# Low weight parts of the late units on VectorE instead of GpSimd

## The chip, the cores and the metric

The kernel runs on one core of a Trainium2 chip. The metric is the device time of one execution in microseconds. A core has TensorE (PE in the profile), VectorE (DVE), ScalarE (ACT), GpSimd (POOL) and SyncE (SP), which here only issues DMA transfers. Each engine works through its own instructions in order and waits on semaphores.

## What is computed

One inference step of a hybrid convolutional decoder layer for 1024 prompt tokens, 16 meta tokens and 8 sample tokens, all in fp32 with a width of 1024:

```
proj = rmsnorm(h) @ w_in                 # 1024 -> 9 * 1024 columns
u_a  = a_val * sigmoid(a_glu);  c_a = layernorm(causal_conv31(u_a) + bias)
y_a  = silu(c_a) * silu(a_gate)
u_b  = b_c * b_h;               y_b = b_b * causal_conv3(u_b) * silu(b_gate)
merged = sigmoid(m_a) * (y_a @ w_pa) + sigmoid(m_b) * (y_b @ w_pb)
h = h + merged @ w_out;         y = rmsnorm(h)
```

## The kernel before

**Units.** The projections are cut into 44 units of 256 output columns: unit 0, then eight rounds of "glu", "short" and "gate" (units 1 to 24), the late units 25 to 35 (gates whose results go to DRAM), "pb" units 36 to 39 (y_b @ w_pb) and "pa" units 40 to 43 (y_a @ w_pa). After them comes the output projection (L2173).

**Seven products.** A unit's 2 x 2 block product over halves of rows, columns and the sum is done as a Strassen-Winograd form with seven products instead of eight, called slots 0 to 6. Each product has 24 matmuls, since each fp32 operand is split into a high part (rounded to fp32r) and a low part (what the rounding left), and high x high, high x low and low x high are summed. The results are evacuated and combined by ScalarE (L1103, L1133, L1148) and VectorE: `c11` (L1664), `c22` (L1670), `c12` (L1675) and `after_c21`.

**Weights.** Six steps n = 0 to 5 prepare the weights of a unit v during unit v - 1: step n makes the high part on ScalarE (`w_hi`, L980, once the slot's product of the unit before is done) and the low part on GpSimd (`w_lo`, L913: raw minus high, 128x512, and 128x1024 for n = 3, which fills slots 3 and 4). The raw blocks lie in `ring`: rb11, rb21, rb22 are loaded (L448, L456, L473), and u1 to u4 are sums. Up to unit 26 the sums are made by accumulating DMAs that GpSimd issues; from unit VSUM = 27 on VectorE makes them in `weight_sum` (L1657). Each low part counts up the semaphore `wlo`, on which TensorE waits before a slot, and SyncE before it loads a ring buffer again.

**Order on SyncE.** All loads and spills stand in one hand-written queue. In a pb unit u (m = u - 36) its order is: u13 of unit u + 2 (L438), spills of the last unit (L620, L624; the latter waits for `after_c21` of that unit), `load_sgb(m, 0)` (L603), rb11 (L448, waits for `wlo` of step 0 of unit u + 1), `load_sg2` (L608), rb21 (L456, waits for step 1), `load_sgb(m, 1)` (L603), a spill, `load_sgb(m, 2)` (L603, waits until the buffer was read), rb22 (L473, waits for step 4), a spill (L616).

**Sigmoids of pb units.** ScalarE copies each sgb load into PSUM (`stage_sigmoids`, L1170) and stands in order between its other work: stage (m, 0) before the third product's evacuation (L1133), stage (m, 1) before the fourth's (L1148). VectorE multiplies with them in `after_c11` (L1682), `after_c22` (L1696) and `after_c12` (L1720). TensorE's slot 4 waits for L1133, slot 5 for L1148, slot 6 for `c22`.

**Phase changes.** Around units 35/36 and 39/40 the moving operand changes as well: ScalarE makes high parts (L996), and VectorE sums (`x_sum`, L1499) and low parts (`x_low`, L1462).

Of the kernel before, what the change touches and what calls it, by code (L numbers as in the profile page):

```python
# [34 lines left out]
def decoder_step(nc, x_prompt, x_sample, state_conv_a, state_conv_b, meta_tokens, norm_g, w_in, conv_a_w,  # L35
# [37 lines left out]
    NZ, NPB, NU = 36, 40, 44  # L73
# [29 lines left out]
    def w_at(v, n):  # L103
        return n + 1 if v == 0 else 6 * v - 2 + n + 1
# [8 lines left out]
    VSUM = LATE0 + 2  # L113
# [4 lines left out]
    def ring_at(v):  # L118

        return v // 2 + v % 2  # L120
# [52 lines left out]
    with ExitStack() as ctx:  # L173
# [6 lines left out]
        def sem(name):  # L180
            return ctx.enter_context(nc.semaphore(name))
# [65 lines left out]
        def f(ap):  # L247
            return ap.bitcast(F32)
# [39 lines left out]
        whi, wlo, prod, snap, ev = sem("whi"), sem("wlo"), sem("prod"), sem("snap"), sem("ev")  # L288
# [66 lines left out]
        def w_step(v, n):  # L355

            if v == 0:
                s = (0, 1, 3, 5)[n]
                return (rb11, rb21, u13[0][:, 0, :], rb22)[n].unsqueeze(1), s, s + 1
            if n == 3:  # L360
                return u13[v % 2], 3, 5
            s = (0, 1, 2, None, 5, 6)[n]
            return (rb11, rb21, u2, None, rb22, u4)[n].unsqueeze(1), s, s + 1
# [513 lines left out]
        @block.gpsimd  # L877
        def _(pool):
            G = nc.gpsimd
            G.memset(eps[:, 0:1], RMS_EPS)  # L880
            G.memset(eps[:, 1:2], LN_EPS).then_inc(pool_const, 1)
            G.memset(ident[:, :], 0.0).then_inc(pool_const, 1)
            G.memset(ones[:, :], 1.0 / D).then_inc(pool_const, 1)
            pool.wait_ge(pool_const, 3)
            G.affine_select(out=ident[:, :], in_=ident[:, :], compare_op=ALU.not_equal, fill=1.0, base=0,
                            pattern=[[-1, P]], channel_multiplier=1).then_inc(pool_const, 1)


            def u1_sum(v):
                pool.wait_ge(rb11_in, 16 * (v + 1))  # L890
                pool.wait_ge(u13_in[v % 2], u13_at(v))
                G.dma_start(u13[v % 2][:, 0, :], rb11, accum_op=ALU.add).then_inc(a1[v % 2], 16)  # L892

            def u2_sum(v):
                pool.wait_ge(u2_in, 16 * v)
                pool.wait_ge(a1[v % 2], 16 * ring_at(v))
                G.dma_start(u2, u13[v % 2][:, 0, :], accum_op=ALU.add).then_inc(a2, 16)  # L897

            def u3_sum(v):
                pool.wait_ge(rb22_in, 16 * (v + 1))  # L900
                pool.wait_ge(u13_in[v % 2], u13_at(v))
                G.dma_start(u13[v % 2][:, 1, :], rb22, accum_op=ALU.add).then_inc(a3[v % 2], 16)

            def u4_sum(v):
                pool.wait_ge(u4_in, 16 * v)
                pool.wait_ge(a2, 16 * v)
                G.dma_start(u4, u2, accum_op=ALU.add).then_inc(a4, 16)

            def w_lo(v, n):

                pool.wait_ge(whi, w_at(v, n))
                raw, s0, s1 = w_step(v, n)
                G.tensor_tensor(wop[:, s0:s1, 1, :], raw, f(wop[:, s0:s1, 0, :]), ALU.subtract).then_inc(wlo, 1)  # L913

            for n in range(4):
                w_lo(0, n)

            u1_sum(1)
            u3_sum(1)
            u2_sum(1)  # L920
            u4_sum(1)
            u1_sum(2)
            u2_sum(2)
            pool.wait_ge(wlo, w_at(1, 5))

            for u in range(1, NU):
                v = u + 1
                if u > 1:
                    w_lo(u, 5)
                if v < NU:  # L930
                    w_lo(v, 0)
                if v < VSUM:
                    u3_sum(v)
                if v < NU:
                    w_lo(v, 1)
                if v < VSUM:
                    u4_sum(v)
                if v < NU:
                    w_lo(v, 2)
                if v + 1 < VSUM:  # L940
                    u1_sum(v + 1)
                if v < NU:
                    w_lo(v, 3)
                if v + 1 < VSUM:
                    u2_sum(v + 1)
                if v < NU:
                    w_lo(v, 4)


# [491 lines left out]
        def _(dve):  # L1441
# [56 lines left out]
                                     (q[0], q[3], q[0], ALU.subtract), (q[1], q[0], q[1], ALU.add))[n]  # L1498
                V.tensor_tensor(out, x, y, op).then_inc(xsum, 1)  # L1499

            def w_low(n):

                dve.wait_ge(whi, w_at(1, n))
                raw, s0, s1 = w_step(1, n)
                V.tensor_tensor(wop[:, s0:s1, 1, :], raw, f(wop[:, s0:s1, 0, :]), ALU.subtract).then_inc(wlo, 1)

            normalize(0)
# [129 lines left out]
            def weight_sum(v, n):  # L1637

                u1, u3 = u13[v % 2][:, 0, :], u13[v % 2][:, 1, :]
                if n == 0:  # L1640
                    dve.wait_ge(rb11_in, 16 * (v + 1))
                    dve.wait_ge(u13_in[v % 2], u13_at(v))
                    dve.wait_ge(wlo, w_at(v - 2, 3))
                    if v - 2 < VSUM:
                        dve.wait_ge(a2, 16 * (v - 2))
                else:
                    dve.wait_ge(usum, usum_at(v, (0, 0, 0, 1)[n]))
                if n == 1:
                    dve.wait_ge(rb22_in, 16 * (v + 1))
                    dve.wait_ge(wlo, w_at(v - 1, 2))  # L1650
                    if v - 1 < VSUM:
                        dve.wait_ge(a4, 16 * (v - 1))
                if n == 3:
                    dve.wait_ge(rb21_in, 16 * (v + 1))
                    dve.wait_ge(wlo, w_at(v - 1, 5))
                out, x, y = ((u1, rb11, u3), (u2, u1, rb22), (u3, u3, rb22), (u4, u2, rb21))[n]
                V.tensor_tensor(out, x, y, ALU.add).then_inc(usum, 1)  # L1657
# [69 lines left out]
            def after_c21(u):  # L1727
                kind, i = UNITS[u]
                if kind in ("short", "pb", "pa"):
                    dve.wait_ge(prod, prod_at(u, 6))  # L1730
                b = psum_half(u, 6)
                if kind == "glu":
                    dve.wait_ge(glu_ready, 2 * i + 2)
                    dve.wait_ge(ev, snap_at(u, 2))
                    if i == 0:
                        dve.wait_ge(xlo, 12)
                        V.memset(ua[:, 0:LEAD], 0.0).then_inc(lead_zero, 1)
                        dve.wait_ge(lead_zero, 1)
                    else:
                        dve.wait_ge(conv_step, CONV_OPS * i)  # L1740
                        dve.wait_ge(conv_act, 3 * i)
                        dve.wait_ge(tail_ready, 2 * i)
                        dve.wait_ge(sa_in, 2 * i)
                    V.tensor_tensor(ua[:, LEAD:LEAD + ALL], g0, g1, ALU.mult).then_inc(ua_ready, 1)
                elif kind == "short":
                    dst = half(g3, u, 1)
                    V.tensor_tensor(dst, b, dst, ALU.mult).then_inc(ub_ready, 1)
                elif kind == "gate":
                    dve.wait_ge(bswish_ready, 2 * i + 2)
                    dve.wait_ge(yb_step, 2 * i + 1)  # L1750
                    V.tensor_tensor(g2[:, META:ALL], g2[:, META:ALL], g0[:, META:ALL], ALU.mult).then_inc(yb_step, 1)
                elif kind == "pb":
                    dst = g3[:, HY:TOK].rearrange("p (c w) -> p c w", w=CY)
                    dve.wait_ge(sg2_in, 16 * i + 16)
                    V.tensor_tensor(dst, b, dst, ALU.mult).then_inc(pb_step, 1)
                elif kind == "pa":
                    halves = [t[:, HY:TOK].rearrange("p (c w) -> p c w", w=CY) for t in (merged_pair(i), old_pair(i))]
                    merge(u, 3, halves[0], b, halves[1])
# [54 lines left out]
            for u in range(1, NU):  # L1813
                kind, i = UNITS[u]
                n = late(u)
# [8 lines left out]
                    w_low(5)  # L1824
                if u > 1:
                    after_c21(u - 1)
                if VSUM <= u + 1 < NU:
                    weight_sum(u + 1, 0)
                if kind == "gate":
# [26 lines left out]
                if VSUM <= u + 1 < NU:  # L1856
                    for step in (1, 2, 3):
                        weight_sum(u + 1, step)
                if kind == "gate":
                    sample_b(i)  # L1860
                if spread:
# [43 lines left out]
                if u == LAST:  # L1905
                    wo_low(3)
                after_c22(u)
                if kind == "short":
                    sample_a(i)
                if spread:  # L1910
# [12 lines left out]

                c12(u)
                after_c12(u)
                if spread:
                    conv_a(cb, steps[2], steps[3])
                    if steps[3] == CONV_OPS:
                        c_sum(cb)
# [287 lines left out]
```

## Time and profile before

| | |
|---|---|
| median of 3 runs | 1082.22 us (1081.83 to 1085.32) |
| the profiled execution | 1079.23 us |
| its span, first to last instruction | 1077.4 us |
| TensorE busy | 1027.6 us, 95% of the span |
| VectorE busy | 838.0 us, 78% |
| GpSimd busy | 521.6 us, 48% |
| ScalarE busy | 469.3 us, 44% |

A row of a timeline gives the start, the time taken, engine, line, operation, output and input, and in brackets how long the engine stood idle before it and what ended that. SPq is SyncE's queue. "x24" is the number of instructions that a row merges; one product has 24 matmuls. An idle time "<-issue" is one whose releaser the profile doesn't name.

### The profile page before, as it was taken

Reading aid. Unit: us, or ns where it says so; the run is one execution under the profiler, and the core shown is the slowest. Engines: PE = TensorE matmul, PEld = TensorE weight load, DVE = VectorE, ACT = ScalarE, POOL = GpSimd, SP = SyncE. Lnnn points to the kernel's source line nnn. Section 1 sums busy time; section 2 is a strip of 40 time slices with the busy share of each in tenths; the row PEclk is TensorE's granted clock in tenths of the full one; section 3 lists DMA queues with packets and bytes.
Section 4 is the critical chain, followed back from the end, with each engine's and each line's share of the span. In section 5 each row is a group of like instructions: output and inputs, shape, how many; then the busy total and the mean of one; then the engine's idle time right before and its main releaser. Section 6 shows DMA issues by size and latency. Waiting matters only on the chain.

```text
span 1077.4 us, 19843 instructions
## 1 busy us (share of the span) xinstructions
PE 1027.6 (95%) x7948; PEld 998.9 (93%) x7948; DVE 838.0 (78%) x904; ACT 469.3 (44%) x723; POOL 521.6 (48%) x369
## 2 busy tenths in 40 slices
PE   5899999999999999999999998999977988999997
PEld 5899999999999999999999998999977988998885
DVE  6779989898998989899995765884784489865523
ACT  7663344434334443433444554565543354232411
POOL 3166566565666665656655553555554455420000
PEclk9999999999999999999999999999989999999999
DMA  8677576656756756666664553766646535455321
GB/s 266 175 166 172 148 176 161 160 140 174 163 144 171 173 142 159 174 144 166 164 167 158 187 184 122 244 228 215 239 144 220 188 119 203 155 193 176 117 80 40
DMA packets 183535, 181.03 MB, mean 168 GB/s; under 512 B 9135, under 2 KB 145455, under 8 KB 182404
## 3 DMA queue, kind: packets, MB, share of 16 engines
q1 hardware_dynamic: 168468, 152.50, 44.1%
q0 software_dynamic: 14976, 27.27, 14.0%
q8 instruction: 63, 1.03, 0.4%
q14 instruction: 28, 0.23, 0.1%
HBM read 118.46 MB, written 35.00 MB: 142 GB/s over the span
## 4 chain that ended last, share of the span: by engine, by line
PE 81%; DVE 7%; issue 4%; DMA 3%; ACT 3%; SPq 1%; POOL 1%; DVEq 0%; ACTq 0%
PE pp L2013 70%; PE pp L2173 8%; DMA sgb<-m_spill 3%; DVE xop L1462 1%; DVE ring L1657 1%; PE pp L2030 1%; DVE big L1499 1%; PE spare L2189 1%; POOL wop L913 1%; DVE big L1941 1%; ACT wop L1012 1%; ACT wop L980 1%; DVE x_stage L1451 1%; DMA x_stage<-in_x_prompt_dram 1%; ACT xop L996 1%
## 5 line engine op out<-in xcount | busy, mean ns | idle before, releaser
L2013 PE MATMUL pp<-xop,wop 128*128 128x262 f32 (+1 forms) x7224 | 893.4, 285 | 27.6 <-ACT big L1133 10.8
L2013 PEld LDWEIGHTS pp<-xop,wop 128*128 128x128 f32 x7224 | 885.9, 190 | 33.1 <-issue 27.2
L913 POOL TENSOR_TENSOR wop<-ring,wop 128x512 fp32r<-128x512 f32 (+1 forms) x256 | 445.2, 1743 | 397.1 <-ACT wop L980 389.8
L980 ACT ACTIVATE wop<-ring 128x512 fp32r<-128x512 f32 (+1 forms) x262 | 182.0, 699 | 238.5 <-PE pp L2013 230.5
L1568 DVE SCALAR_TENSOR_TENSOR big<-big,cst 128x513 f32<-128x513 f32 x112 | 108.7, 971 | 0.8
L2173 PE MATMUL pp<-xop,wop 128*128 128x512 f32 x384 | 89.2, 394 | 0.0
L2173 PEld LDWEIGHTS pp<-xop,wop 128*128 128x128 f32 x384 | 72.0, 188 | 16.8
L1579 DVE SCALAR_TENSOR_TENSOR spare<-big,tap_sum,spare 128x512 f32<-128x512 f32 x112 | 83.9, 749 | 0.3
L1568 DVE SCALAR_TENSOR_TENSOR spare<-big,cst,spare 128x512 f32<-128x512 f32 x112 | 83.7, 747 | 0.0
L1670 DVE TENSOR_TENSOR big<-big,pp 128x524 f32<-128x524 f32 (+1 forms) x43 | 29.9, 695 | 49.6 <-PE pp L2013 34.8
L1657 DVE TENSOR_TENSOR ring<-ring 128x512 f32<-128x512 f32 x68 | 66.0, 1010 | 0.0
L1675 DVE TENSOR_TENSOR big<-pp,big 128x524 f32<-128x524 f32 (+1 forms) x43 | 29.9, 696 | 34.9 <-PE pp L2013 34.9
L1133 ACT ACTIVATE big<-pp 128x524 f32<-128x524 f32 (+1 forms) x43 | 26.1, 607 | 66.5 <-PE pp L2013 62.5
L1462 DVE TENSOR_TENSOR xop<-big,xop 128x2064 fp32r<-128x2064 f32 (+1 forms) x18 | 53.2, 2974 | 2.0 <-ACT xop L996 2.0
L1664 DVE TENSOR_TENSOR big<-pp,big 128x524 f32<-128x524 f32 (+1 forms) x43 | 30.0, 698 | 31.4 <-PE pp L2013 31.4
L1103 ACT ACTIVATE big<-pp 128x524 f32<-128x524 f32 (+1 forms) x43 | 26.1, 607 | 63.4 <-PE pp L2013 63.4
L996 ACT ACTIVATE xop<-big 128x2064 fp32r<-128x2064 f32 (+1 forms) x18 | 34.6, 1927 | 4.9 <-DVE big L1499 4.9
L1148 ACT ACTIVATE big<-pp 128x524 f32<-128x524 f32 (+1 forms) x43 | 25.7, 597 | 23.3 <-PE pp L2013 23.3
L1499 DVE TENSOR_TENSOR big<-big 128x2064 f32<-128x2064 f32 (+1 forms) x12 | 31.3, 2611 | 0.0
L892 POOL DMA_DIRECT2D ring<-ring x26 | 23.2, 891 | 15.9 <-DMA ring<-in_w_in_dram 15.9
L1290 ACT ACTIVATE y_stage<-y_stage 128x1024 f32<-128x1024 f32 (+1 forms) x9 | 9.6, 1062 | 45.7 <-DVE y_stage L1969 39.6
L897 POOL DMA_DIRECT2D ring<-ring x26 | 22.5, 864 | 13.6 <-DMA ring<-ring 11.4
(126 smaller groups left out, 715.4 us busy)
## 6 DMA issues: line engine op xcount, KB each, us to landing
ring<-in_w_in_dram SPq DMA_DIRECT2D x222, 256.0 KB, 3.4
ring<-ring POOLq DMA_DIRECT2D x104, 256.0 KB, 4.5
big<-c_spill SPq DMA_DIRECT2D x16, 516.0 KB, 5.4
big<-yb_spill SPq DMA_DIRECT2D x5, 1032.0 KB, 8.2
big<-ya_spill SPq DMA_DIRECT2D x5, 1032.0 KB, 7.7
m_spill<-big SPq DMA_DIRECT2D x16, 262.0 KB, 4.3
yb_spill<-big SPq DMA_DIRECT2D x8, 516.0 KB, 5.4
c_spill<-big SPq DMA_DIRECT2D x8, 516.0 KB, 4.6
```

What stands on the lines that cost most here:

```text
L913: G.tensor_tensor(wop[:, s0:s1, 1, :], raw, f(wop[:, s0:s1, 0, :]), ALU.subtract).then_inc(wlo, 1)
L980: A.activation(wop[:, s0:s1, 0, :], raw, ACT.Copy).then_inc(whi, 1)
L996: A.activation(xview(p, s, 0), x_src(p, s), ACT.Copy).then_inc(xhi, 1)
L1462: V.tensor_tensor(xview(p, s, 1), x_src(p, s), f(xview(p, s, 0)), ALU.subtract).then_inc(xlo, 1)
L1499: V.tensor_tensor(out, x, y, op).then_inc(xsum, 1)
L1568: ins = V.scalar_tensor_tensor(out=out, in0=u(tap, n), scalar=const(j, tap), in1=out, op0=ALU.mult, op1=ALU.add)
L1579: ins = V.scalar_tensor_tensor(out=acc_s, in0=acc_u[:, i:i + HALF], scalar=tap_sum[:, j, i:i + 1], in1=acc_s if i else odd, op0=ALU.mult, ...
L1657: V.tensor_tensor(out, x, y, ALU.add).then_inc(usum, 1)
L1664: V.tensor_tensor(dst, psum_half(u, 1), dst, ALU.add).then_inc(ev, 1)
L1670: V.tensor_tensor(dst, dst, psum_half(u, 4), ALU.subtract).then_inc(ev, 1)
L2013: last = T.matmul(out, wop[:, s, wp, P * k:P * (k + 1)], xop[s][:, xp, k, n * ch:n * (ch + 1)], start=(s in FRESH and k == 0 and m == 0), ...
L2173: last = T.matmul(pp[(t + 2) % 3][:, h, :], tile_op(t, xp)[:, k, :], xop[2 * h + wp][:, k // KH, k % KH, 0:512], start=(k == 2 and m == 0) ...
```

## The change

The low parts of units 27 to 43 are made on VectorE. GpSimd's loop ends with unit 26. On VectorE step 5 of unit u stands behind `after_c21(u - 1)`, and for unit u + 1 steps 0 and 1 stand behind the weight sums, steps 2 and 3 behind `after_c22(u)`, and step 4 behind `after_c12(u)`.

```diff
-            for u in range(1, NU):
+            for u in range(1, VSUM):
                 v = u + 1
                 if u > 1:
                     w_lo(u, 5)
-                if v < NU:
+                if v < VSUM:
                     w_lo(v, 0)
...
-            def w_low(n):
+            def w_low(n, v=1):
-                dve.wait_ge(whi, w_at(1, n))
-                raw, s0, s1 = w_step(1, n)
+                if v == VSUM and n == 0:
+                    dve.wait_ge(wlo, w_at(v - 1, 5))
+                dve.wait_ge(whi, w_at(v, n))
+                raw, s0, s1 = w_step(v, n)
                 V.tensor_tensor(wop[:, s0:s1, 1, :], raw, f(wop[:, s0:s1, 0, :]), ALU.subtract).then_inc(wlo, 1)
...
                 if u > 1:
                     after_c21(u - 1)
+                if u >= VSUM:
+                    w_low(5, u)
...
                     for step in (1, 2, 3):
                         weight_sum(u + 1, step)
+                    w_low(0, u + 1)
+                    w_low(1, u + 1)
...
                 after_c22(u)
+                if VSUM <= u + 1 < NU:
+                    w_low(2, u + 1)
+                    w_low(3, u + 1)
...
                 after_c12(u)
+                if VSUM <= u + 1 < NU:
+                    w_low(4, u + 1)
```

## Rows read from the trace of the kernel before

**Rows 1.** The page: busy time of each engine.

```profile
PE 1027.6 (95%) x7948; PEld 998.9 (93%) x7948; DVE 838.0 (78%) x904; ACT 469.3 (44%) x723; POOL 521.6 (48%) x369
```

**Rows 2.** Who TensorE waited for, 560 to 975 us: total, times, longest.

```profile
PE pp L2013 <- ACT big L1133: 9.7, 3, 6.3
PE pp L2013 <- ACT big L1148: 6.2, 4, 2.4
PE pp L2013 <- issue: 6.0, 3, 2.6
```

**Rows 3.** Groups by line and shape on VectorE, 640 us to the end.

```profile
L1657 DVE TENSOR_TENSOR ring<-ring 128x512 f32<-128x512 f32 x55 | 53.3, 1009 | 0.0
L1462 DVE TENSOR_TENSOR xop<-big,xop 128x2064 fp32r<-128x2064 f32 x14 | 43.2, 3105 | 1.3 <-ACT xop L996 1.3
...
L1777 DVE TENSOR_TENSOR big<-big 128x1032 f32<-128x1032 f32 x8 | 15.7, 1967 | 0.0
```

**Rows 4.** Single lines: least, median and most ns of one instruction.

```profile
L1657 DVE TENSOR_TENSOR ring<-ring x68: 676/683/1798, 571.8 to 942.8; 128x512 f32<-128x512 f32 x68
L1505 DVE TENSOR_TENSOR wop<-ring,wop x6: 686/688/1221, 49.8 to 62.6; 128x512 fp32r<-128x512 f32 x5, 128x1024 fp32r<-128x1024 f32 x1
L1462 DVE TENSOR_TENSOR xop<-big,xop x14: 2296/3383/3878, 774.4 to 906.4; 128x2064 fp32r<-128x2064 f32 x14
L913 POOL TENSOR_TENSOR wop<-ring,wop x106: 1282/1692/3672, 560.0 to 954.9; 128x512 fp32r<-128x512 f32 x88, 128x1024 fp32r<-128x1024 f32 x18
```

**Rows 5.** The chain that ended last, in order of time, around unit 36's start.

```profile
784.88 2.97 POOL wop L913
787.87 0.37 SPq L473
...
788.84 2.34 SPq L438
...
795.58 4.87 DMA sgb<-m_spill
...
804.07 4.68 PE pp L2013 x24
```

**Rows 6.** Timeline around the end of unit 36.

```profile
815.99 0.69 DVE L1720 TENSOR_TENSOR big<-big,spare 128x516 f32<-128x516 f32 x1
816.53 0.38 SPq L473 DMA_DIRECT2D ring<-in_w_pb_dram  x1
```

**Rows 7.** Timeline of units 37 and 38.

```profile
835.40 20.52 PE L2013 MATMUL pp<-xop,wop 128*128 128x258 f32 x168 [2.35 <-ACT big L1148]
...
840.67 0.37 SPq L473 DMA_DIRECT2D ring<-in_w_pb_dram  x1
...
843.11 0.69 DVE L1720 TENSOR_TENSOR big<-big,spare 128x516 f32<-128x516 f32 x1 [3.83 <-ACT spare L1170]
...
844.81 0.46 SPq L603 DMA_DIRECT2D sgb<-m_spill  x1
...
846.96 0.38 SPq L448 DMA_DIRECT2D ring<-in_w_pa_dram  x1
...
852.62 0.51 SPq L603 DMA_DIRECT2D sgb<-m_spill  x1
...
857.35 2.90 PE L2013 MATMUL pp<-xop,wop 128*128 128x258 f32 x22 [1.42 <-ACT big L1148]
```

**Rows 8.** Timeline from unit 39's `c22` to unit 40.

```profile
883.75 0.68 DVE L1670 TENSOR_TENSOR big<-big,pp 128x516 f32<-128x516 f32 x1
...
896.76 3.40 DVE L1462 TENSOR_TENSOR xop<-big,xop 128x2064 fp32r<-128x2064 f32 x1
...
900.25 3.12 PE L2013 MATMUL pp<-xop,wop 128*128 128x258 f32 x24 [0.95 <-issue]
...
905.97 39.19 PE L2013 MATMUL pp<-xop,wop 128*128 128x258 f32 x310 [2.60 <-issue]
```

**Rows 9.** Stretches of TensorE: length, busy, granted clock, DMA share, GB/s.

```profile
650.00:652.00 2.00, 0.00 (x0) 1.00 0.00 0
...
654.00:656.00 2.00, 2.00 (x12) 0.50 0.00 0
...
875.00:877.00 2.00, 0.00 (x0) 1.00 0.00 0
```

**Rows 10.** Bytes moved at DMA share 1: stretches in unit 38's load burst.

```profile
845.00:846.00 1.00, 1.00 (x11) 1.00 1.05 384
```

More of the change, by code:

```diff
@@ L929, in _ @@
                     w_lo(u, 5)
-                if v < NU:
+                if v < VSUM:
                     w_lo(v, 0)
-                if v < VSUM:
                     u3_sum(v)
-                if v < NU:
                     w_lo(v, 1)
-                if v < VSUM:
                     u4_sum(v)
-                if v < NU:
                     w_lo(v, 2)
@@ L941, in _ @@
                     u1_sum(v + 1)
-                if v < NU:
+                if v < VSUM:
                     w_lo(v, 3)
@@ L945, in _ @@
                     u2_sum(v + 1)
-                if v < NU:
+                if v < VSUM:
                     w_lo(v, 4)
```

## The prediction

> **What bounds the kernel now.** I read the page first: TensorE is busy for 95% of the span, GpSimd for 48% [rows 1]. So the 521.6 us of GpSimd cost nothing by themselves; the change pays only where TensorE stands still. Next the view of who waits for whom, for the units that it touches (560 to 975 us). TensorE waits there for the evacuation of the third product (9.7 us), for that of the fourth (6.2 us) and for things that the profile doesn't name (6.0 us) [rows 2]. It waits for no low weight part by name. Last, the chain of waits shows what stands behind the longest of these (6.3 us, at the start of unit 36): a low part on GpSimd (2.97 us), SyncE's queue, a load of sgb, ScalarE, TensorE [rows 5]. In the four pb units the sgb loads set the pace, and SyncE's queue sets when they leave. At the phase change from 39 to 40 it is VectorE: it goes without a pause from `c22` at 883.75 on, and slots 4 and 5 of unit 40 start when its x_low end (idle 0.95 and 2.60 us) [rows 8].
>
> **What is removed and added.** On VectorE a low part takes 0.69 us, the wide one 1.22 [rows 4]. A unit gets 5 x 0.69 + 1.22 = 4.7 us, 17 units 79 us. Against this, VectorE's own work between two SBUF tensors becomes shorter. A weight sum takes 0.683 us as a median, 1.009 on average in this stretch; an x_low 2.30 at least, 3.11 on average; L1777's mean is 1.97 where, by length, 1.23 would be expected (an estimate: 2.30 x 1032/2064 plus a fixed 0.08) [rows 3, 4]. The long ones are those that overlap a GpSimd low part, itself 1.28 to 3.67 us. Over the 55 sums this is 18 us, over the 14 x_low 11 us, over L1777 6 us, and with the same share on lines like them (L1499, L1687, L1689, L1785) I put the whole at 50 to 58 us. VectorE gains about 20 us of work net, 1.2 us a unit of 20.5. In the late units 27 to 35 it has that room: the PE products go on for 2.9 us each, and the evacuations wait for TensorE, not for VectorE. I take nothing there but +0.2 us at unit 30, where the reciprocal (6.6 us) and the normalizations already hold TensorE, and -0.5 at the end of unit 35, where `c22` is late behind x_low and comes 0.8 us earlier.
>
> The Trainium skill, SBUF — State Buffer, section "Who interferes with whom", says that a DVE instruction with two SBUF inputs and a GpSimd instruction that reads SBUF exclude each other for a whole instruction. The trace agrees: 0.683 against up to 1.798 us. By that page alone, everything is gain for both engines.
>
> **The pb units, on the path.** Times are shifts against the trace.
> 1. First sgb load. It stands behind rb22 (L473, 787.87), which waits for step 4. On VectorE, with x_low and x_sum shorter, step 4 ends some 0.7 us earlier: -0.7.
> 2. sgb(0, 1). rb11 and sg2 left before unit 36's stage 0; now rb11 waits for step 0, which stands behind `c11`, `after_c11` (waits for that stage) and three sums. So rb11 (256 KB) and sg2 (258 KB) leave directly ahead of rb21 and sgb(0, 1). At 384 GB/s [rows 10] they take 1.4 us; the issues add 0.3. Steps 0 and 1 (1.3 us) replace what the three sums lose in contention. +1.7, in all +1.0.
> 3. Step 4 of unit 37. It stands behind `after_c12` (815.99): 0.62 + 0.65 later is 817.3, where rb22 left at 816.53 [rows 6]. With the shift from 2, rb22 leaves 1.5 us later than before: +0.5.
> 4. sgb(1, 1). The DMA engines are full then with the big loads of the next operand, so order matters little: -0.3.
> 5. Step 4 of unit 38, the dearest. `after_c12(37)` waits for a stage until 843.11, while GpSimd had done step 4 before, and rb22 left at 840.67 [rows 7]. Now step 4 ends at about 843.1 + 0.6 + 0.65 = 844.4, and rb22, spill, u13, spill, spill (5 issues of 0.45 us, 2.3 us) stand ahead of sgb(2, 0): 846.7 instead of 844.81, +1.9. These five and the sgb load are 1.55 MB in one burst, 4.0 us at 384 GB/s, so it lands another 0.9 later. +2.8, in all +4.0.
> 6. sgb(2, 1): rb11 ahead of it as in 2 (before it left at 846.96, 5.7 us ahead of the load at 852.62). Part of this lay in the burst: +0.5. Slot 5 of unit 38 starts 4.5 us later than at 857.35; its wait grows from 1.42 to about 4.8 us, as slot 4 itself moves by 1.2.
> 7. The clock. An idle time of 3.9 us near 650 left TensorE at 0.50 in the stretch after it, 1.2 instead of 2.4 GHz; the 2.2 us near 876 left it at 1.00 [rows 9]. A product at the low level takes 4.5 us instead of 2.9: +1.6, if it falls. In all +6.1.
> 8. Units 39 and 40. VectorE goes from `c22(39)` to the end of x_low for slot 4 in 16.4 us [rows 8]. It gets four low parts (3.1 us) and loses 3.9 of contention; and TensorE, being late itself, no longer waits 0.95 and 2.6 us in full: -1.8, in all +4.3. Without step 7 it is +4.5 - 1.7 = +2.8.
>
> In the pa units step 4 stands behind six multiplications and additions, and rb11 holds the load of the old sums (L644) about 3.5 us longer. That load has roughly 7 us of transfer and was needed about 8 us after it left; `merge_two` would wait 1 to 2 us, and `c12` has 1.4 us of room before slot 1 of the next unit, plus the 3 us by which the merges shorten. I take 0; if that cover is gone it costs 1 to 2 us in each of two units. The output projection is untouched: 0.
>
> **Sum.** +2.8 to +4.3, with the 0.2 of unit 30 +3.0 to +4.5. I take +4.0, as the idle time in 6 is longer than the one that lowered the clock. The profiled execution would go from 1079.2 to 1083.2; its time is 3.0 us under the median, and I add the same to the median: 1082.2 + 4.0 = 1086.2 us. 0.3% is 3.2 us, about what a measurement of this kernel can tell from no change.
>
> **Rivals.**
> - *The queue moves, but the path hardly does* (chance 0.28). The bursts of steps 2 and 5 overlap with idle DMA engines, the clock holds, and 8 gives more back: 0 to +2, some 1083.3 us. For it: the sgb loads after 865 land in a slack stretch. Against it: slot 5 stands directly behind them in all four units.
> - *Faster: the freed port wins* (0.07). This is the page's rule as a mechanism here: steps 1 and 8 carry on. L438's 2.34 us in front of the first sgb load [rows 5] falls away (-2.3), x_low at 2.30 instead of 3.4 gives -0.5 at unit 35 and -1.0 at unit 40: -3.8, 1078.4 us. It decides if sgb(2, 0) leaves before about 845.5; against it is the order of step 4 behind `after_c12`.
> - *More waits* (0.15). The cover in the pa units is gone (+3) and the clock falls twice (+1.6): +8.5, some 1090.5 us.
> - *The forecast* (0.50): +2.8 to +5.5.
>
> Slower by over 0.3%: 0.15, and 0.40 of the 0.50; same: the rest of it, 0.28 less a little; faster 0.07. Range: the rivals' middle parts, 1081.6 to 1090.5.
>
> **What would show it.** L913 ends near 590 us; L1657's mean is 0.68, x_low's 2.3. rb22 (L473) in units 36 to 38 leaves behind L1720 and a low part, five SyncE issues stand in a row ahead of L603, rb11 and sg2 directly ahead of the second sgb load. TensorE's wait for L1148 grows from 6.2 us to over 10. I am wrong if these waits stay near 6 us, or if VectorE's `c22` and `c12` in the late units come later than TensorE allows.

## The result and the profile after

The changed kernel took 1087.72 us as a median of 20 runs (1082.81 to 1093.44), the kernel before 1081.81 us (20 runs, 1078.98 to 1085.32). The two medians differ by 5.9 us, where 4.0 were forecast. The measured ratio is 1.0063, with a 95% interval of 1.0048 to 1.0077: slower by 0.63%, or 6.8 us. The profiled execution took 1087.04 us with a span of 1085.2, 7.8 us longer than that of before. Of these 7.8 us some 2 lie in the choice of executions: the one of before was 2.6 us under its kernel's median, this one 0.7 under its own.

The page of the changed kernel, busy time of each engine, and below it who TensorE waited for from 560 to 985 us:

```profile
PE 1031.3 (95%) x7948; PEld 1002.9 (92%) x7948; DVE 845.6 (78%) x1006; ACT 468.9 (43%) x723; POOL 328.2 (30%) x267
```

```profile
PE pp L2021 <- ACT big L1145: 12.7, 4, 6.1
PE pp L2021 <- ACT big L1130: 10.2, 3, 5.9
PE pp L2021 <- issue: 3.4, 3, 1.4
```

GpSimd lost 193 us of work. VectorE got 79 us (85 narrow and 17 wide low parts), and its busy time rose by only 7.6 us [rows 1]. Added up by their durations, its other instructions became 64 us shorter: 52 us from 640 us on, and 12 us between 560 and 640. The rest is overlap: a VectorE instruction of 0.69 us often starts some 0.07 us before the one ahead of it has ended (842.18 and 842.79 below), and busy time counts that only once. TensorE's wait for the fourth product (L1148 before, L1145 now) doubled from 6.2 to 12.7 us; that for the third hardly moved (9.7 to 10.2), and the unnamed one fell from 6.0 to 3.4 [rows 2].

Groups by line and shape on VectorE, from 640 us to the end. L1504 is the low part, L1656 the weight sum, L1459 x_low, L1776 the subtraction that was L1777:

```profile
L1504 DVE TENSOR_TENSOR wop<-ring,wop 128x512 fp32r<-128x512 f32 x70 | 46.8, 685 | 3.4 <-ACT wop L977 3.3
L1656 DVE TENSOR_TENSOR ring<-ring 128x512 f32<-128x512 f32 x55 | 35.3, 684 | 0.0
L1459 DVE TENSOR_TENSOR xop<-big,xop 128x2064 fp32r<-128x2064 f32 x14 | 31.9, 2300 | 0.0
...
L1776 DVE TENSOR_TENSOR big<-big 128x1032 f32<-128x1032 f32 x8 | 9.8, 1227 | 0.0
```

The stretching is gone in these rows: the sums went from 1009 to 684 ns, x_low from 3105 to 2300, L1777 from 1967 to 1227 [rows 3].

The timeline around the end of unit 36, then of units 37 and 38, for the rows that answer to [rows 6, 7]:

```profile
815.95 0.69 DVE L1719 TENSOR_TENSOR big<-big,spare 128x516 f32<-128x516 f32 x1
816.56 0.68 DVE L1504 TENSOR_TENSOR wop<-ring,wop 128x512 fp32r<-128x512 f32 x1
817.27 0.38 SPq L473 DMA_DIRECT2D ring<-in_w_pb_dram  x1
...
836.05 20.48 PE L2021 MATMUL pp<-xop,wop 128*128 128x258 f32 x168 [3.02 <-ACT big L1145]
...
842.18 0.69 DVE L1719 TENSOR_TENSOR big<-big,spare 128x516 f32<-128x516 f32 x1 [2.28 <-ACT spare L1167]
842.79 0.68 DVE L1504 TENSOR_TENSOR wop<-ring,wop 128x512 fp32r<-128x512 f32 x1
843.50 0.37 SPq L473 DMA_DIRECT2D ring<-in_w_pb_dram  x1
843.92 0.51 SPq L616 DMA_DIRECT2D mb_spill<-big  x1
844.47 0.43 SPq L438 DMA_DIRECT2D ring<-in_w_pa_dram  x1
844.95 0.66 SPq L620 DMA_DIRECT2D mb_spill<-big  x1
845.65 0.45 SPq L624 DMA_DIRECT2D mb_spill<-big  x1
846.14 0.43 SPq L603 DMA_DIRECT2D sgb<-m_spill  x1
850.95 0.61 ACT L1167 ACTIVATE spare<-sgb 128x516 f32<-128x516 f32 x1 [4.79 <-DMA sgb<-m_spill]
...
854.07 1.29 DVE L1504 TENSOR_TENSOR wop<-ring,wop 128x512 fp32r<-128x512 f32 x2
854.78 0.38 SPq L448 DMA_DIRECT2D ring<-in_w_pa_dram  x1
855.21 0.50 SPq L608 DMA_DIRECT2D big<-m_spill  x1
855.82 0.39 SPq L456 DMA_DIRECT2D ring<-in_w_pa_dram  x1
856.25 0.50 SPq L603 DMA_DIRECT2D sgb<-m_spill  x1
861.32 0.60 ACT L1167 ACTIVATE spare<-sgb 128x516 f32<-128x516 f32 x1 [7.70 <-DMA sgb<-m_spill]
...
862.59 9.70 PE L2021 MATMUL pp<-xop,wop 128*128 128x258 f32 x56 [6.06 <-ACT big L1145]
```

Read it from the top: the multiplication with the sigmoids waits for ScalarE, the low part of step 4 stands behind it, and only then does rb22 (L473) leave, with four more issues before the sgb load. The load is ready at 850.95, where it was at 847.85 before (the stage L1170 in that trace). Then the two low parts of steps 0 and 1 end, and rb11, sg2 and rb21 go directly ahead of the second sgb load, which leaves at 856.25 and is ready at 861.32: 5.1 us, where it had taken 3.5 (852.62 to 856.08). TensorE stands still for 6.06 us instead of 1.42.

Stretches of TensorE in the changed kernel: length, busy, granted clock, DMA share, GB/s.

```profile
858.00:860.00 2.00, 0.00 (x0) 0.63 0.86 283
...
864.00:866.00 2.00, 2.00 (x11) 0.50 0.03 10
...
886.00:888.00 2.00, 2.00 (x11) 0.50 1.04 296
```

The granted clock fell to 0.50, 1.2 GHz, during this wait, and slot 5 of unit 38 took 5.5 us (862.59 to the evacuation at 868.12) instead of 2.9. It fell once more at unit 39. In both kernels it had also fallen during the wait of some 6 us at unit 36.

### The profile page after: what moved, and what is told of

Same layout as the page of the kernel before. It is cut to its first block, busy times and chain, and to the rows that moved or that the text cites. A ratio compares the mean times of both kernels' runs of the same rounds, so it can differ in the third digit from the quotient of the medians.

```text
span 1085.2 us, 19844 instructions
## 1 busy us (share of the span) xinstructions
PE 1031.3 (95%) x7948; PEld 1002.9 (92%) x7948; DVE 845.6 (78%) x1006; ACT 468.9 (43%) x723; POOL 328.2 (30%) x267
## 4 chain that ended last, share of the span: by engine, by line
PE 83%; DVE 6%; DMA 5%; ACT 3%; issue 2%; SPq 1%; DVEq 0%; ACTq 0%
PE pp L2021 72%; PE pp L2181 8%; DMA sgb<-m_spill 4%; DVE wop L1504 1%; PE pp L2038 1%; DVE big L1496 1%; DVE ring L1656 1%; PE spare L2197 1%; DVE xop L1459 1%; DMA x_stage<-in_x_prompt_dram 1%; DVE big L1949 1%; ACT wop L1009 1%; DVE x_stage L1448 1%; ACT spare L1167 0%; DMA m_spill<-big 0%
## 5 line engine op out<-in xcount | busy, mean ns | idle before, releaser
L2021 PE MATMUL pp<-xop,wop 128*128 128x262 f32 (+1 forms) x7224 | 897.2, 286 | 30.9 <-ACT big L1145 12.7
L913 POOL TENSOR_TENSOR wop<-ring,wop 128x512 fp32r<-128x512 f32 x154 | 252.5, 1646 | 206.5 <-ACT wop L977 203.1
L1504 DVE TENSOR_TENSOR wop<-ring,wop 128x512 fp32r<-128x512 f32 x108 | 80.7, 774 | 4.6 <-ACT wop L977 4.5
L1674 DVE TENSOR_TENSOR big<-pp,big 128x524 f32<-128x524 f32 (+1 forms) x43 | 29.9, 696 | 20.0 <-PE pp L2021 19.9
L1656 DVE TENSOR_TENSOR ring<-ring 128x512 f32<-128x512 f32 x68 | 44.8, 700 | 0.0
L1459 DVE TENSOR_TENSOR xop<-big,xop 128x2064 fp32r<-128x2064 f32 (+1 forms) x18 | 41.9, 2348 | 0.8 <-ACT xop L993 0.7
L1145 ACT ACTIVATE big<-pp 128x524 f32<-128x524 f32 (+1 forms) x43 | 25.6, 596 | 23.7 <-PE pp L2021 23.6
L1625 DVE SCALAR_TENSOR_TENSOR big<-big,cst 128x1024 f32<-128x1024 f32 x16 | 27.8, 1738 | 0.6
L1496 DVE TENSOR_TENSOR big<-big 128x2064 f32<-128x2064 f32 (+1 forms) x12 | 27.8, 2314 | 0.0
```

The lines of the kernel that those rows point to most:

```text
L1459: V.tensor_tensor(xview(p, s, 1), x_src(p, s), f(xview(p, s, 0)), ALU.subtract).then_inc(xlo, 1)
L2021: last = T.matmul(out, wop[:, s, wp, P * k:P * (k + 1)], xop[s][:, xp, k, n * ch:n * (ch + 1)], start=(s in FRESH and k == 0 and m == 0), ...
```

## Experiments

Each was run beside the kernel before on the same chip, but not all on one chip, so runs of different experiments are compared by their ratios. *Queue theory*: the loss comes from where steps 0 and 4 stand on VectorE, because SyncE's queue waits for them with the sgb loads behind. *Load theory*: VectorE has too much to do. Ratios are against the kernel before.

**x1: step 4 ahead of `after_c12`.**

```diff
-                after_c12(u)
                 if VSUM <= u + 1 < NU:
                     w_low(4, u + 1)
+                after_c12(u)
```

> The changed kernel, with step 4 ahead of after_c12 instead of behind it; nothing else. Queue theory: rb22 in unit 37 leaves near 840.2 instead of 843.5, so four of the five transfers are out of the way of sgb(2, 0), which leaves near 844.9 instead of 846.1 and lands near 848; TensorE's wait for the fourth product in unit 38 falls from 6.06 to 3 to 4 us, and the time falls by 3 to 5 us against the changed kernel, to 1.0015 to 1.0035 of the kernel before. Load theory (VectorE simply has too much to do): the same work stands on VectorE, so the time stays at 1.005 to 1.008.

1.0015 (0.9997 to 1.0034), 1083.78 us. TensorE's wait in unit 38 fell from 6.06 to 2.88 us. In this run slot 5 of unit 37 started when it did in the changed kernel (836.02) but ended later, as the granted clock was 0.57 to 0.58 from 836 to 840 (VectorE's evacuation of it, L1674, at 840.69 instead of 839.20). rb22 left at 842.13, directly behind that and step 4, and ahead of the multiplication (842.17). The first sgb load left at 844.75 and was ready at 849.24 instead of 850.95. The second, still behind rb11, sg2 and rb21, left at 854.68 and was ready at 859.63, 5.0 us later. So half of the wait in unit 38 went with step 4, as the queue theory had it; x2 tests the order that is left, with step 0. Over all four pb units the wait for the fourth product hardly fell in the profiled execution (12.7 to 12.5 us: 3.14, 3.62, 2.88 and 2.84), and it was the one for the third that did (10.2 to 6.1).

**x2: step 0 ahead of `after_c11` and the sums.**

```diff
+                if VSUM <= u + 1 < NU:
+                    w_low(0, u + 1)
                 after_c11(u)
                 if VSUM <= u + 1 < NU:
                     for step in (1, 2, 3):
                         weight_sum(u + 1, step)
-                    w_low(0, u + 1)
                     w_low(1, u + 1)
```

> The changed kernel, with step 0 ahead of after_c11 and the three weight sums (step 1 stays behind them). Queue theory: rb11 and sg2 leave 3 to 5 us ahead of the second sgb load of each pb unit instead of directly ahead of it, so this load lands 1 to 1.5 us sooner after it leaves; 1 to 3 us less than the changed kernel, 1.003 to 1.005 of the kernel before. Load theory: 1.005 to 1.008, as changed.

0.9991 (0.9974 to 1.0007), 1080.86 us: 0.7% under the changed kernel, more than expected. Its timeline has rb11 8 us ahead of the second sgb load in unit 38, and that load is ready 3.4 us after it leaves:

```profile
846.08 0.70 SPq L448 DMA_DIRECT2D ring<-in_w_pa_dram  x1
...
854.12 0.51 SPq L603 DMA_DIRECT2D sgb<-m_spill  x1
857.53 0.60 ACT L1167 ACTIVATE spare<-sgb 128x516 f32<-128x516 f32 x1 [5.01 <-DMA sgb<-m_spill]
```

Step 4 still stands where it does in the changed kernel, and TensorE's wait in unit 38 is still 4.04 us.

**x3: both moves.**

> Both moves together. Queue theory: the sgb loads leave and land within 0.5 us of the kernel before or earlier, the clock holds as before, and the gains at the ends of units 35 and 40 are left over: 0.997 to 1.001 of the kernel before. Load theory: 1.005 to 1.008.

0.9917 (0.9897 to 0.9937), 1073.03 us. The work on VectorE is that of the changed kernel, and yet it is 1.5% faster than that, and faster than the kernel before by more than expected. TensorE in units 36 to 40:

```profile
807.16 3.10 PE L2022 MATMUL pp<-xop,wop 128*128 128x258 f32 x24 [0.89 <-ACT big L1145]
...
831.97 18.28 PE L2022 MATMUL pp<-xop,wop 128*128 128x258 f32 x137 [1.76 <-ACT big L1145]
854.45 17.59 PE L2022 MATMUL pp<-xop,wop 128*128 128x258 f32 x144 [0.47 <-ACT big L1145]
872.67 17.55 PE L2022 MATMUL pp<-xop,wop 128*128 128x258 f32 x141 [0.63 <-ACT big L1130]
```

Against [rows 7], slot 5 is 3.4 us earlier in unit 37 and 2.9 in unit 38. With the steps out of the way, what is left on the path (stage, multiplication, three sums, step 1, the second sgb load) is shorter than before: the three sums of unit 38 take 1.89 us where they took 2.96. I had counted that gain as used up. How much of the 9 us comes from it is not shown by this run.

**x4: GpSimd keeps all the work, but waits as VectorE would.**

```diff
             def w_lo(v, n):
+                kind, m = UNITS[v - 1]
+                if v >= VSUM and n == 0:
+                    pool.wait_ge(usum, usum_at(v, 3))
+                if n == 4 and kind == "pb":
+                    pool.wait_ge(pb_step, 4 * m + 3)
+                if n == 4 and kind == "pa":
+                    pool.wait_ge(pa_step, 8 * m + 6)
                 pool.wait_ge(whi, w_at(v, n))
```

> The kernel before, all low parts on GpSimd, but from unit 27 on GpSimd's step 0 waits until the weight sums of its unit are done, and its step 4 in pb and pa units waits for after_c12. VectorE gets no work. Queue theory: the sgb loads come late as in the changed kernel, and VectorE keeps its contention as well: 1.006 to 1.014. Load theory: VectorE has what it had before, so 0.998 to 1.002.

1.0210 (1.0187 to 1.0233), 1105.07 us: beyond the range of the queue theory. Late steps lose time with no moved work at all, so the load theory, with 0.998 to 1.002, is excluded as the whole cause. TensorE's waits, from 560 to 1000 us:

```profile
PE pp L2020 <- ACT big L1155: 21.3, 4, 6.1
PE pp L2020 <- ACT big L1140: 10.9, 3, 7.0
```

L1155 is the fourth product: 21.3 us where it was 6.2 [rows 2]. The late steps cost 23 us here. That is not the price of the order in the changed kernel: a low part takes 1.92 us on GpSimd in this run (the mean of the narrow ones) and 0.69 on VectorE, so each step here ends later than in the changed kernel, and VectorE's own work stays stretched.

**x5: the kernel before with another order on SyncE**, the sgb loads ahead of the ring loads.

```diff
+                if u == NZ:
+                    load_sgb(0, 0)
                 if kind == "pb":
-                    load_sgb(i, 0)
+                    load_sgb(i, 1)
...
                 if kind == "pb":
-                    load_sgb(i, 1)
                     spill_pb1(i)
...
                     load_sgb(i, 2)
+                if kind == "pb" and i < 3:
+                    load_sgb(i + 1, 0)
```

> The kernel before (low parts on GpSimd) with another order on SyncE: load_sgb(m, 1) stands ahead of rb11 instead of behind rb21, and load_sgb(m + 1, 0) ahead of rb22 instead of behind the next unit's spills. Queue theory: the sgb loads no longer wait for low parts at all, so TensorE's waits for L1133 and L1148 in units 37 to 39 (7.2 us before) nearly vanish: 0.992 to 0.996 of the kernel before. If the loads' time on the DMA engines is what counts and not the order: 0.999 to 1.002.

0.9951 (0.9929 to 0.9972), 1075.42 us, as the queue theory had it: the queue cost the kernel before as well. No wait for the third or fourth product is left in units 37 to 39.

**x6: x3 and x5 together.**

> x3_both_first with the order on SyncE of x5_before_sgb_first as well. Queue theory: what x3 gained came from the same waits, so most of it can't be had twice; 0.988 to 0.992, at or a little under x3's 0.9917. If the order on VectorE gave its gain by itself: 0.984 to 0.988.

0.9899 (0.9881 to 0.9918), 1069.75 us, within the queue theory's range: less than the 1.3% that x3 and x5 would give if they added. x5 and x6 ran on one chip and have the same order on SyncE, so the 5.7 us between them (1075.42 to 1069.75) are what the moved low parts are worth once the queue no longer holds the sgb loads. This is the whole of the move, shorter low parts and shorter VectorE work together. In x5's profile TensorE waits 4.2 us for VectorE's `c22`, in x6's it doesn't.

**x7 and x8: the change for a part of the units.** A test in `w_lo` and `w_low` decides by unit which engine makes the low part, with one wait on `wlo` where it changes over: `VSUM <= v <= NZ` on VectorE in x7, `v > NZ` in x8.

> VectorE makes the low parts of units 27 to 36 as in the changed kernel, GpSimd those of 37 to 43 as in the kernel before. Queue theory: no step 0 or 4 of units 37 to 40 stands behind a sigmoid stage, and the phase change at unit 35 gains up to 1.2 us; 0.997 to 1.000. Load theory: ten of seventeen units keep the load, 1.003 to 1.005.

> The other part: GpSimd makes the low parts of units 27 to 36, VectorE those of 37 to 43. Queue theory: all of the loss is here, and the first load's 1.2 us are missing: 1.006 to 1.009. Load theory: 1.002 to 1.004.

x7: 0.9984 (0.9971 to 0.9998), 1078.63 us. x8: 1.0086 (1.0063 to 1.0108), 1090.25 us. Added, -0.16% and +0.86% give +0.70%, beside the +0.63% of the whole change. All of the loss is in the low parts of units 37 to 43, and those of units 27 to 36 gain a little.

**x9: x3 with each moved low part made twice.**

```diff
+                if v > 1:
+                    V.tensor_tensor(wop[:, s0:s1, 1, :], raw, f(wop[:, s0:s1, 0, :]), ALU.subtract).then_inc(twice, 1)
+                    dve.wait_ge(twice, 6 * (v - VSUM) + n + 1)
                 V.tensor_tensor(wop[:, s0:s1, 1, :], raw, f(wop[:, s0:s1, 0, :]), ALU.subtract).then_inc(wlo, 1)
```

> x3_both_first with each moved low part made twice on VectorE, one after the other, with the same result; this adds 4.9 us of work a unit to VectorE and nothing else. Queue theory: TensorE doesn't wait for VectorE except at the phase changes, so 2 to 5 us more than x3: 0.994 to 0.997 of the kernel before. Load theory: VectorE is near its limit, and doubling the moved work costs much more than moving it: over 1.005.

1.0233 (1.0213 to 1.0252), 1105.27 us: a miss. Some 80 us of further work on VectorE cost 3.2% against x3, some 34 us. From 680 to 780 us VectorE is busy for 92%, where it was 72% in x3, and TensorE now waits for it by name:

```profile
PE pp L2026 <- DVE big L1673: 4.9, 3, 1.9
PE pp L2026 <- DVE xop L1460: 4.2, 1, 4.2
```

The waits for the third and fourth product grew as much (7.6 to 11.1 us and 3.1 to 10.0), since every step on the path to the sgb loads is longer too. So this run doesn't separate the two theories. It shows that VectorE had room for about the work that it got, not for twice that; that the load is not what made the change as made slower is shown by x3 and x12, which carry the same load.

**x10: x3 with GpSimd kept reading.**

```diff
+            for v in range(VSUM, NU):
+                for n in (0, 1, 2, 3, 4, 5):
+                    pool.wait_ge(whi, w_at(v, n))
+                    for _ in range(5 if n == 3 else 3):
+                        G.tensor_tensor(st_raw[:, :, :], ones[:, :].unsqueeze(1).broadcast_to([P, 2, P]),
+                                        ones[:, :].unsqueeze(1).broadcast_to([P, 2, P]), ALU.subtract).then_inc(idle, 1)
...
```

> x3_both_first with GpSimd kept reading: from unit 27 on it does 3 subtractions of 128x256 from a constant into an unused buffer at each high part (5 at the wide one), about the time of the low parts it had; nothing waits for them. VectorE's sums and low parts stretch again. If x3's gain of 9 us comes from the freed port alone: 0.999 to 1.003. Queue theory: the earlier places of steps 0 and 4 keep part of it, and the stretched sums and x_low take the rest: 0.994 to 0.999.

1.0227 (1.0205 to 1.0249), 1104.95 us, outside both ranges, and not a fair test of size. From 680 to 780 us GpSimd was busy for 91%, not the 56% of the kernel before: its filler took 1.07 us each. The groups on VectorE, from 640 us on:

```profile
L1516 DVE TENSOR_TENSOR wop<-ring,wop 128x512 fp32r<-128x512 f32 x71 | 60.3, 850 | 1.4 <-ACT wop L989 1.3
L1668 DVE TENSOR_TENSOR ring<-ring 128x512 f32<-128x512 f32 x56 | 56.9, 1055 | 0.0
```

The sums are at 1055 ns, near the 1009 of before [rows 3], and the low parts at 850 instead of 684. It shows the direction: with both the moved work and a stretched VectorE, which is busy for 92% there, the gain is gone and more. How much of x3's 9 us is the port's by itself stays open.

**x11: x6 with the first sgb load in unit 35.** The waits for all the late spills move to `load_sgb(1, 0)`.

```diff
                 n, last_n = late(u), late(u - 1)
+                if u == NZ - 1:
+                    load_sgb(0, 0)
...
                 if m == 0 and n == 0:
-                    sp.wait_ge(lp1_out, 16 * LATES)
-                    sp.wait_ge(lp2_out, 16 * LATES)
+                    sp.wait_ge(lp1_out, 16 * (LATES - 1))
+                    sp.wait_ge(lp2_out, 16 * (LATES - 2))
```

> x6_both_sgb_first with the first sgb load issued at the top of unit 35, before that unit's own spills, since the data it reads was spilled ten units before. TensorE's 4.5 us wait at slot 4 of unit 36 should go, and the low clock after it: 5 to 8 us under x6, 0.983 to 0.986 of the kernel before. If something else is as late there (rb11, the moving operand): 0.987 to 0.990.

0.9841 (0.9819 to 0.9862), 1063.62 us: the fastest of all, 1.6% under the kernel before and 2.2% under the changed one. The long wait of [rows 5], 6.3 us, is gone; what is left there are waits of 1.52 and 2.17 us:

```profile
799.65 0.59 PE L2028 MATMUL pp<-xop,wop 128*128 128x258 f32 x3 [1.52 <-DVE xop L1465]
804.93 35.27 PE L2028 MATMUL pp<-xop,wop 128*128 128x258 f32 x290 [2.17 <-issue]
```

**x12: the changed kernel as it is, with SyncE's order of x5.**

> The changed kernel as it is on VectorE (step 4 behind after_c12, step 0 behind the sums), with SyncE's order of x5. Queue theory: the late steps hold rb11 and rb22 but no longer any sgb load, so nearly all of the loss goes and the freed port is left: 0.990 to 0.995. If the late steps hurt in another way than through the sgb loads: 1.000 to 1.004.

0.9915 (0.9895 to 0.9935), 1070.44 us. Steps 0 and 4 are as late as in the changed kernel; only the sgb loads no longer stand behind them, and the loss has turned into a gain of 0.85%. If SyncE's order only added x5's own gain to the changed kernel, the ratio would be 1.001 (1.0063 x 0.9951), as in the expectation's second case; it is 1% under that. With x4 this settles the cause from both sides: late steps without moved work lose, moved work with late steps but free sgb loads wins.

## Why the prediction was right, point by point

The direction, the place and the mechanism held. The median, 1087.72, lies 1.5 us above the forecast of 1086.2 and within the range. The sum came so near in part by luck, as steps 2 to 5 were too dear and steps 6 and 7 too cheap. In shifts of the profiled execution against the trace of before:

| step | forecast | measured |
|---|---|---|
| unit 30 | +0.2 | +0.3 (673.61 to 673.80, 645.33 to 645.22 ahead of it) |
| 1, first sgb load leaves | -0.7 | -1.0 (795.58 to 794.55) |
| 2, slot 5 of unit 36 | +1.0 | +0.1 (809.90 to 809.98) |
| 3, rb22 in unit 36 | +1.5 | +0.7 (816.53 to 817.27) |
| 5, sgb(2, 0) leaves | +3.1 (1.2 + 1.9) | +1.3 (844.81 to 846.14) |
| 5, sgb(2, 0) is ready | +4.0 | +3.1 (847.85 to 850.95) |
| 6, slot 5 of unit 38 | +4.5 | +5.2 (857.35 to 862.59) |
| 7, slot 5 of unit 39 | +6.1 | +10.4 (881.57 to 891.94) |
| 8, output projection starts | +4.3 | +7.8 (974.22 to 982.01) |

*What bounds the kernel* held: not GpSimd's 48%, but SyncE's queue in the pb units. x5 shows it without any moved work.

*VectorE's balance*: +20 us forecast, +15 measured by durations (79 less 64), +7.6 by busy time. The estimate of 50 to 58 us was made from rows from 640 us on, and there it held (52 us). It left out the 12 us between 560 and 640, in units 27 to 29.

The Trainium skill's rule in SBUF — State Buffer, section "Who interferes with whom", agrees with the trace: with GpSimd silent, the 14 x_low took 2298 to 2302 ns, where they had been 2296 to 3878 [rows 4]. The prediction's remark that by this rule alone everything would be gain came true only when the queue was mended (x3, x12).

*Steps 2 and 3* were too dear. The first sgb load was ready 1.3 us earlier (800.47 to 799.21) and not 0.7, and the second took 4.2 us to be ready instead of 3.4 (804.50 to 808.71; 805.27 to 808.63), 0.8 more where 1.4 were taken. Step 3 inherits that.

*Step 4* was left at +0.65 (slot 5 of unit 37, 835.40 to 836.05) instead of +1.2. The issue of the u13 load (L438) in unit 37 took 0.43 us instead of 1.92, and so sgb(1, 0) left 0.6 us earlier than before and sgb(1, 1) when it had left before (829.90, 829.92). I call that luck: nothing that the change does explains it, and the same issue took 1.22 us in x1 and 1.08 in x2. The two rows, before and after:

```profile
817.50 1.92 SPq L438 DMA_DIRECT2D ring<-in_w_pb_dram  x1
...
818.25 0.43 SPq L438 DMA_DIRECT2D ring<-in_w_pb_dram  x1
```

*Step 5* had the order right and the start wrong. The multiplication in front of step 4 came not 1.2 us later but 0.9 earlier (843.11 to 842.18), since sgb(1, 2) was ready 6.1 us after it left instead of 7.6; why, no run here shows. From rb22 to the sgb load it took 2.6 us, 2.3 forecast. Then the load was ready 4.8 us after it left instead of 3.0: +1.8, where 0.9 were taken for the burst.

*Step 6* was too cheap, by 1.6 us: the second load was ready 5.1 us after it left, directly behind rb11, sg2 and rb21, and 3.5 us in the trace before. Only +0.5 was put down for this, as a part was thought to lie in the burst of step 5, but that burst was over: sgb(2, 0) was ready at 850.95, the DMA share was 0 from 851 to 855, and rb11 left at 854.78. This made TensorE's wait 6.06 us instead of 4.8.

*Step 7 is where the sum fell short.* I counted one product at the low level, +1.6. The granted clock fell to 1.2 GHz during the longer wait, at about 858.5, and stayed there through the whole of slot 5 and into slot 6 (2.9 us together: 8.8 us from 862.59 to 871.41, where two products take 5.9), and again at slot 4 of unit 39 (4.62 us instead of 3.13, +1.5). That is 4.4 us in all, 2.8 more than forecast. The two waits of unit 39 were 1.0 us longer besides (2.84 and 1.58 us instead of 2.23 and 1.23). One reading of the prediction was also off: the idle time near 650 was 3.07 us, not 3.9. Over the 20 runs the mean clock went from 0.989 in the fastest (1082.81 us) to 0.980 in the slowest (1093.44 us), so this part differs from run to run. That the clock follows the waits was seen; it was not tried by itself.

*Step 8* gave back 2.6 us (10.4 to 7.8) instead of 1.8. A part of this was not in the sum: in the trace before, slot 5 of unit 40 ran at a granted clock of 0.50 (907 to 909) and took 4.7 us to its evacuation at 910.63, after the change it ran at 1.00. The pa units cost 0 as taken: from slot 6 of unit 40 to the output projection it is 63.8 us after (918.16 to 982.01), and 63.6 before, from that evacuation on.

*Rivals*: "more waits" got its clock part right and its pa part wrong. "Faster" named the freed port; x3, and x6 against x5, show that the move has a gain, and that the order hid it.

## What to carry to other kernels

A step that is moved to another engine takes its place in that engine's order, and with it whatever waits there; ask for its semaphore which queue waits on it, and what stands in that queue behind the wait. Here 0.7 us instructions placed behind a multiplication that waits for a load delayed the next such load, and TensorE's granted clock fell to 0.50 in the idle time that followed. Put the steps that free buffers ahead of the ones that wait for data, and the loads on the path ahead of those with slack.

## What the runs showed of the hardware

- A VectorE instruction with two SBUF inputs took the same time to 0.2% when GpSimd was silent (x_low 2298 to 2302 ns), and 35% more on average beside GpSimd's low parts (3105 ns). GpSimd work that only reads a constant and writes an unused buffer stretched VectorE's instructions as well (x10: the sums at 1055 ns instead of 684).
- A load's time depends on what left just ahead of it: the same 258 KB of the second sgb load were ready after 3.4 to 4.2 us behind rb21 alone (the four pb units of before), and after 4.2 to 5.1 us behind rb11, sg2 and rb21 (those of the changed kernel).
- The issue of a load on SyncE doesn't always take the same time: L438 in unit 37, always 256 KB, took 1.92 us before, 0.43 in the changed kernel, 1.22 in x1 and 1.08 in x2. What makes it long is not shown.
- The clock doesn't follow from the length of the idle time alone: in the changed kernel one of 6.06 us and, later, one of 2.84 us were each followed by TensorE at 0.50, and one of 3.02 us (unit 37) was not.
